# Values computed by token, modulation sums in the down-projections, operands on 2 KB lines, and the latent attention taken two heads at a time

## What is computed

```python
ckv = rms_norm(h, kv_in_norm) @ w_dkv                  # 256 latent columns and 64 rope columns
kv = rms_norm(c_kv, kv_norm) @ w_ukv                   # 8 heads of 128 key and 128 value columns
s = (q_nope @ k_nope.T + q_rope @ k_rope.T) * scale    # causal, softmax, @ v, @ w_o
```

## Time and profile before

| | |
|---|---|
| median of 3 runs | 1872.62 us (1869.66 to 1875.88) |
| the profiled execution | 1877.21 us |
| its span, first to last instruction | 1875.5 us |
| TensorE busy | 1795.5 us, 96%, 7820 matmuls |
| vector engine, ScalarE, GpSimd busy | 1142.2, 700.9, 405.1 us |
| mean granted TensorE clock | 0.979 |

### The profile page before, as it was taken

The page is one execution under the profiler, slowest core; times in us unless marked ns, Lnnn a source line. Parts: engine busy times, 40 slices in busy tenths (PEclk is TensorE's granted clock), DMA queues, the critical chain, the costliest instruction groups (busy, mean ns, idle before and its releaser), DMA issues.

```text
span 1875.5 us, 22480 instructions
## 1 busy us (share of the span) xinstructions
PE 1795.5 (96%) x7820; PEld 1422.5 (76%) x7820; DVE 1142.2 (61%) x1509; ACT 700.9 (37%) x975; POOL 405.1 (22%) x172
## 2 busy tenths in 40 slices
PE   7978999999999899999999999899999899999997
PEld 6756788888887676778888888688657688888885
DVE  6998877777224765567777522473855667777212
ACT  4112444444223335444444322332463444434221
POOL 3434300000444340120000144344201300000342
PEclk9999999999999999999999999899998899999998
DMA  7565433223333220022232233222100222232231
GB/s 266 212 212 186 172 101 100 97 93 101 101 101 98 67 93 1 32 90 94 99 100 90 97 105 101 94 89 90 56 1 13 78 90 92 98 101 89 102 101 67
DMA packets 52043, 186.32 MB, mean 99 GB/s; under 512 B 5776, under 2 KB 6032, under 8 KB 51856
## 3 DMA queue, kind: packets, MB, share of 16 engines
q1 hardware_dynamic: 50256, 180.90, 28.4%
q10 hardware_dynamic: 1728, 4.63, 0.7%
HBM read 183.41 MB, written 2.10 MB: 99 GB/s over the span
## 4 chain that ended last, share of the span: by engine, by line
PE 81%; DVE 13%; issue 2%; ACT 2%; DVEq 0%; DMA 0%; POOL 0%; ACTq 0%; SPq 0%
PE ps L1429 24%; PE ps L1431 24%; PE ps L1430 24%; DVE ada L966 4%; PE ps L1595 1%; PE ps L1592 1%; DVE TG L978 1%; PE ps L1613 1%; DVE RB L1055 1%; DVE rb L852 1%; PE ps L1649 1%; PE ps L1682 1%; PE ps L1603 1%; DVE acc L848 1%; DVE CU L990 1%
## 5 line engine op out<-in xcount | busy, mean ns | idle before, releaser
L462 POOL TENSOR_TENSOR WL<-raw,WH 128x1024 fp32r<-128x1024 f32 x159 | 394.1, 2479 | 1422.2 <-ACT WH L514 1422.2
L1429 PE MATMUL ps<-XH,WH 128*128 128x512 f32 x1560 | 616.6, 395 | 37.3 <-DVE XL L859 10.5
L1430 PE MATMUL ps<-XL,WH 128*128 128x512 f32 x1560 | 610.4, 391 | 0.0
L1431 PE MATMUL ps<-XH,WL 128*128 128x512 f32 x1560 | 610.3, 391 | 0.0
L514 ACT ACTIVATE WH<-raw 128x1024 fp32r<-128x1024 f32 x291 | 308.2, 1059 | 579.1 <-PE ps L1431 577.2
L1429 PEld LDWEIGHTS ps<-XH,WH 128*128 128x128 f32 x1560 | 294.8, 189 | 110.6 <-issue 19.5
L1431 PEld LDWEIGHTS ps<-XH,WL 128*128 128x128 f32 x1560 | 294.7, 189 | 62.2
L1430 PEld LDWEIGHTS ps<-XL,WH 128*128 128x128 f32 x1560 | 294.9, 189 | 60.9 <-issue 1.0
L1431 PE MATMUL ps<-HH,WL 128*128 128x512 f32 x528 | 208.6, 395 | 0.0
L1429 PE MATMUL ps<-HH,WH 128*128 128x512 f32 x528 | 208.6, 395 | 0.0
L1430 PE MATMUL ps<-HL,WH 128*128 128x512 f32 x528 | 208.5, 395 | 0.0
(11 more groups left out here) (257 smaller groups left out, 1877.5 us busy)
## 6 DMA issues: line engine op xcount, KB each, us to landing
raw<-w_tiles SPq DMA_DIRECT2D x291, 512.0 KB, 3.2
ada<-ada_tiles SPq DMA_DIRECT2D x48, 512.0 KB, 4.5
out_x<-X SPq DMA_DIRECT2D x8, 256.0 KB, 2.2
X<-x_in ACTq DMA_DIRECT2D x2, 512.0 KB, 8.4
X<-x_in SPq DMA_DIRECT2D x2, 512.0 KB, 8.8
MK<-mask_in ACTq DMA_DIRECT2D x1, 1024.0 KB, 4.8
crow<-c_in ACTq DMA_DIRECT2D x1, 512.0 KB, 11.5
cst<-const_in ACTq DMA_DIRECT2D x1, 384.0 KB, 13.2
```

The costliest lines, as they stand in the source:

```text
L462: nc.gpsimd.tensor_tensor(WL[k % SPL][:, :], raw[:, k, :], f32(WH[k % SPL][:, :]), ALU.subtract).then_inc(s_lo, 1)
L1429: mm(bank, h, xh, start=first, stop=False)
L1430: mm(bank, h, xl, start=False, stop=False)
L1431: return mm(bank, lo, xh, start=False, stop=last)
```

## The change

- Each value product has the activations as weights and the weight tile as the moving operand (`token_dot`, `token_group`), so that its result stands by token; `to_aux`, `turn`, `take` and `take_v` go. In UKV the first two tiles are keys, the last two values. In IN2 the first eight tiles are two groups of four banks with 512 columns, the next two (IN2R) one group of 256 columns, whose weights are read at a stride of four tokens. The four copies of a group come at its end.
- The modulation's loads and sums go to DN0 and DN1, three per chunk, in three slots; `crow` and the rope tables use other buffers and are loaded by SyncE when those are free. The operations on `mod` and `gm` follow DN1.
- The small buffers are allotted first, and the operands of the split products start on multiples of 2 KB.
- The attention takes heads 2j and 2j + 1 alternately. At an even step TensorE issues QN KN and mask of both blocks, then both rope products.

```diff
-ADA = 6
+ADA = 3
+LINE = 4 * S
-    ("IN2", 22, [1]), ("OUT2", 8, [1]), ...
+    ("IN2", 8, [0, 0, 0, 4]), ("IN2R", 2, [0, 4]), ("IN2F", 12, [1]), ("OUT2", 8, [1]), ...
-        XH = sb("XH", [P, KD, S], F32R)
+        XH = sb("XH", [P, KD, S], F32R, align=LINE)
...
-        HH = sb("HH", [P, FF, S], F32R, st)
+        HH = sb("HH", [P, FF, S], F32R, st, align=LINE)
...
+        ADA_SLOT = (ada01[:, 0, :], ada01[:, 1, :], trig[:, :, :].rearrange("p a b -> p (a b)"))
+        crow = RAB[:, :, :].rearrange("p a b -> p (a b)")
...
+        def block_a(a):
+            return a // 8 * 2 + a % 2, a % 8 // 2
...
+            def load_ada(n, m):
+                if m == 0:
+                    sp.wait_ge(s_hl, FF * (n + 1))
+                else:
+                    sp.wait_ge(s_ada, ADA * (KD * n + m))
+                for q in range(ADA):
+                    sp.dma_start(ADA_SLOT[q], ada_tiles[ADA * (KD * n + m) + q]).then_inc(s_ada_in[q], 16)
...
+                for n in range(2):
+                    down = t - T0[f"DN{n}"]
+                    if down == 5:
+                        load_ada(n, 0)
+                    elif down >= 6 and down % 3 == 0 and down <= 3 * KD:
+                        load_ada(n, down // 3 - 1)
...
             def head_hi(h):
-                act.wait_ge(s_pv, 4 * h + 4)
+                act.wait_ge(s_pv, h // 2 * 8 + 7 + h % 2)
...
-                if a % 4 == 0 and a >= 8:
-                    head_hi(a // 4 - 2)
+                if a % 8 in (3, 4) and a >= 8:
+                    head_hi(a // 8 * 2 - 2 + a % 8 - 3)
...
                     for k in range(4):
                         m, M = i * 4 + k, M0[phase] + k
+                        if modulation is not None:
+                            adaln(modulation, i, k)
                         product(M, i, per)
...
-                if a % 4 == 1 and a >= 9:
-                    head_lo(a // 4 - 2)
+                if a % 8 in (4, 5) and 8 <= a < BLOCKS_A:
+                    head_lo(a // 8 * 2 - 2 + a % 8 - 4)
+            head_lo(HEADS - 2)
             head_lo(HEADS - 1)
...
+            def token_dot(bank, t, blk, width, xh, xl, first, last):
+                h = WH[t % SPL][:, blk * width:(blk + 1) * width]
+                lo = WL[t % SPL][:, blk * width:(blk + 1) * width]
+                mm(bank, xh, h, start=first, stop=False)
+                mm(bank, xl, h, start=False, stop=False)
+                return mm(bank, xh, lo, start=False, stop=last)
...
+                if a < BLOCKS_A and a % 2 == 0:
+                    for c in (a, a + 1):
+                        h, qb = block_a(c)
+                        L, bank = (qb + 1) * P, ps[SB[c % 4]]
+                        if c >= 4:
+                            pe.wait_ge(s_p, c - 3)
+                        mm(bank[:, 0:L], QN[:, h, qb * P:L], KN[:, h, 0:L], start=True, stop=False)
+                        mm(bank[:, L - P:L], mask16[:, 0, :], mask16[:, 1, :], start=False, stop=False, ...)
+                    for c in (a, a + 1):
+                        h, qb = block_a(c)
+                        L, half, bank = (qb + 1) * P, h % 2 * HD, ps[SB[c % 4]]
+                        mm(bank[:, 0:L], QR[half:half + HD, h // 2, qb * P:L], KR[half:half + HD, 0:L],
+                           start=False, stop=True).then_inc(s_s, 1)
...
                     if qb == 0 and h >= 2:
                         pe.wait_ge(s_ol, h - 1)
...
             for k in range(n_in):
+                if k in (0, 4):
+                    token_group(T0["IN2"] + k, M0["IN2"] + k, 4, S, block_of, inputs(E_M2) if k == 0 else None)
+                elif k == 8:
+                    token_group(T0["IN2R"], M0["IN2R"], 2, 2 * P, class_of)
+                elif k >= N_TOK:
+                    wide(T0["IN2F"] + k - N_TOK, M0["IN2F"] + k - N_TOK)
```

More of the change, by code:

```diff
@@ L444, in _ @@
                 load(t)
[L445 to L448, removed]
+                if t == T0["A_OUT"]:
+                    load_crow()
+                if t == T0["UP1"] + RAW:
+                    sp.wait_ge(s_ol, HEADS)
+                    load_crow()
+                for n in range(2):
[4 more added lines that the diff above has]
+                        load_ada(n, down // 3 - 1)
+                if t == T0["DN0"] + 3 * KD + 2:
+                    sp.wait_ge(s_ada, ADA * KD)
+                    for half in range(2):
+                        sp.dma_start(trig[:, half, :], rope_in[half]).then_inc(s_in["rope"], 16)
             for m in range(KD):
@@ L599, in body @@
                         newest_tap(M + 1, i, CU, TU, jj + FF)
+                    if isinstance(i, int) and f < 2:
+                        act.wait_ge(s_in["c"], 16 * (f + 1))
+                        nc.scalar.activation(crow, crow, ACT.Silu).then_inc(s_cact, 1)
                 nc.scalar.preload_act_table(ACT.Silu)
@@ L862, in product, with adaln, residual @@
                 dve.wait_ge(s_pe, i * per + DONE_M[M])
-            def residual(phase, tiles_per_m, e, gname, n, gate=None, beside=None, second=False):
+            def adaln(n, i, k):
+                for q in range(ADA):
+                    a = i * (4 * ADA) + (ADA * (KD * n + k) + q)
+                    dve.wait_ge(s_ada_in[q], i * 64 + 16 * (KD * n + k + 1))
+                    dst = mod[:, a:a + 1] if isinstance(a, int) else mod[:, bass.ds(a, 1)]
+                    w = ADA_SLOT[q]
+                    v.scalar_tensor_tensor(w, w, 1.0, crow, ALU.mult, ALU.mult, accum_out=dst).then_inc(s_ada, 1)
+            def residual(phase, tiles_per_m, e, gname, n, gate=None, modulation=None, second=False):
                 per = 4 * tiles_per_m
@@ L1217, in in_tile @@
             def in_tile(k):
-                M, aux = M0["IN2"] + k, AUX_2 + k
-                if k < N_TOK:
-                    to_aux(aux, M)
+                M = M0["IN2F"] + k - N_TOK
+                if k in (3, 7, 9):
+                    first, dst = ((M0["IN2"], VU), (M0["IN2"] + 4, CB), (M0["IN2R"], CV12))[k // 4]
+                    for n in range(4):
+                        product(first + n)
+                        bank = ps[(first + n) % 4]
+                        v.tensor_copy(dst[:, n, :], bank[:, 0:2 * P] if k == 9 else bank[:, :]).then_inc(s_ev, 1)
+                elif k < N_TOK:
+                    pass
                 elif k < KEYS_AT:
@@ L1561, in _ @@
                         spread(1, ps[4], RA)
-                    if t > 0 and j % 2 == 0:
-                        h = 2 * (t - 1) + j // 2
-                        turn(AUX_V + h, M0["UKV"] + 2 * h + 1)
             for t in range(6):
@@ L1712, in _ @@
                 if k == KEYS_AT:
[L1713 removed]
+                    pe.wait_ge(s_ev, M0["IN2F"] + KEYS_AT - N_TOK)
                 if k >= KEYS_AT:
@@ L1717, in _ @@
             stick(BESIDE + 1)
-            pe.wait_ge(s_ev, M0["IN2"] + n_in)
+            pe.wait_ge(s_ev, M0["OUT2"])
             gated()
@@ L1847, in tiles, with rows_first @@
         return t.reshape(-1, P, TILE)
+    def rows_first(w, cols, width):
+        w = w[:, cols]
+        per = BLK * P // width
+        t = w.reshape(-1, per, P, w.shape[1] // width, width).transpose(3, 0, 2, 1, 4)
+        return t.reshape(-1, P, TILE)
     def interleave(*starts):
```

274 lines of the change are left out of this document (112 added, 162 removed).

## The result

| | before | after |
|---|---|---|
| median | 1873.84 us, 4 runs (1869.66 to 1875.88) | 1842.66 us, 4 runs (1842.36 to 1845.36) |
| the profiled execution | 1877.21 us, span 1875.5 | 1842.36 us, span 1840.6 |
| mean granted TensorE clock | 0.979 | 0.984 |

A forecast was written before the change was run, and what follows sets the result against it. TensorE, busy 96% of the span, was taken as the bound. Terms -31.8 - 10.2 - 1.3 - 3.3 - 4.8 - 3.3 + 1.3 + 6.9 = -46.5 took the profiled 1877.21 to 1830.7, the median to 1826 us; range 1813 to 1840.

The forecast's parts named there:

- Modulation: Layer A: without the vector engine's 48 multiply-accumulates, 28 tiles fall to 152.3 us, -31.8 us; DN0 and DN1 take them at 0.
- rival (d): DN0 and DN1: the moved modulation becomes a ring, at 19.4 us a chunk +93 us, kernel 1919; chance 0.02.
- Alignment: Down-projections: operands on 2 KB lines bring products from 0.233 to 0.2267 us, -10.2 us; WO -1.0, latent products -0.3.
- I take the address for the cause: Down-projections and WO: operands off 2 KB lines explain products at 0.233 us, those on XH at 0.2267.
- Rival (b): Down-projections: alignment isn't the cause of 0.233 us, but place in memory or the operands' writers; kernel 1838; chance 0.14.
- By token: UKV, UQ and IN2 lose copies and transposes: -3.3 us, ten IN2 tiles -4.8, IN2's first tile -3.3.
- The four evictions at a group's end: IN2: evictions come four at once, the next tile wants its first bank 4 us later, cost 0.
- I add 0.01 for the stride: 12.2.: IN2R: 96 half-width products with weights at stride four take 12.2 us, +1.3, bounds +0.6 and +11.7.
- rival (c): IN2R: the strided weight loads set the pace, +10.4 us, kernel 1836; chance 0.08.
- The wait for `s_ol`: Attention: TensorE waits for OL of both heads, 3.3 us at each of three changes of pair, +9.9 us.
- -3.0: Attention: back-to-back rope products each save an unhidden weight load of 0.095 us, two per pair over 16 pairs.
- rival (a): Attention: no wait for `s_ol`, 1816, or both rope products run at once, saving 4.3 us, 1812 at best; chance 0.16.

The follow-up runs named there:

- e7: Kernel before the change, with the 48 modulation products on the vector engine cut from 1024 columns to 8: 1844.03 us, two runs.
- e2: Kernel after the change, with tensors aligned to 2 KB lines moved to the next 32 bytes: 1844.44 us, ratio 0.9856.
- e5: Kernel after the change, with gaps ahead of some tensors so that some operands lie 128 bytes from the weights modulo 256: 1857.11 us.
- e1: Kernel after the change, with IN2R's stationary tile taken from 128 adjacent columns, not every fourth: 1834.94 us, ratio 0.9795.
- e11: Kernel of e4, with IN2R's stationary tile taken from every second column, not every fourth: 1817.35 us against 1828.99.
- e4: Kernel after the change, with high and low halves of a head pair's attention results made earlier: 1828.99 us, ratio 0.9766.
- e12: Kernel of e8, with the 64-row products of a head pair put apart again: 1829.82 us against 1821.23.
- e3: Kernel after the change, with attention back to one head after the other and each 64-row product in its own block: 1841.85 us.
- e6: Kernel of e4, with each block's 64-row product put back behind its own mask product: 1836.59 us against 1828.99.
- e8: Kernel of e4, with IN2R's two tiles done in two products per block instead of three: 1821.23 us, ratio 0.9732.

## Why the prediction was wrong

**Modulation, right.** -33.1 against -31.8, and e7 shows the cause: vector-engine time, not the transfers. The move into DN0 and DN1 cost nothing, as forecast; rival (d) did not come. The room there was larger than the prediction had it: a chunk is 123.1 / 8 = 15.4 us, and 15.0 after, not 14.1 and 13.6, a slip that changed no term.

**Alignment, right in size, wrong in cause.** -10.9 against -10.2. The gain came by luck: a start on a 2 KB line is not what speeds these products up, but it also puts both operands alike modulo 256. The step "I take the address for the cause" had even a wrong fact in it: by the layout given under e2 the six first buffers began 128 bytes behind a 2 KB line. e2 leaves the lines and keeps the gain, e5 takes it back with positions that differ by 128 modulo 256. Rival (b) was right to doubt the lines, and wrong to expect no gain.

**By token, nearly right.** UKV and the latent gave -3.5 against -3.6. IN2's first tile fell from 9.5 to 5.6 us (-3.9 against -3.3). The next seven gave less: TensorE waits 0.5 us in them for GpSimd's low half, and 1.2 for a bank. The four evictions at a group's end, which I had put at 0, were not free.

**The strided load: the first step that failed.** "I add 0.01 for the stride: 12.2." It is 22.5. The value stood as the upper bound, 22.6 from 0.235 each, and rival (c) is this. I took the lower one since strided passes of 64 rows had cost only 0.03 more than packed ones. I compared the passes and not the loads. The loads' own rows were in the trace of before, strided (L1691) and packed (L1595), with busy us and mean ns of one:

```profile
L1691 PEld LDWEIGHTS ps<-FT 64*128 64x128 f32 x32 | 8.6, 320 | 3.1 <-issue 1.8
L1595 PEld LDWEIGHTS ps<-KR,QR 64*128 64x128 f32 x64 | 9.4, 184 | 10.2 <-issue 10.2
```

The loads of IN2R take 330 ns, much like the strided ones here. That a load hides at a pitch of 0.11 us was true of the packed ones alone. The Trainium skill's 16-byte line (SBUF - State Buffer) spoke for the upper bound, and e1 and e11 bear it out. This step is worth 10.3 us.

**The attention: the second.** The wait for `s_ol` was there, 10.4 against 9.9, though its parts were off both ways: the first of a change of pair took 2.10 us where I had 1.5, the second 1.05 to 1.53 where I had 1.7 to 1.8. Missing was what the wait does to the clock: the earlier trace rows had 1.00 in that stretch, and I priced two idle times, of 1.5 and 1.8 us, as idle times alone. The 7.8 us are shown by e4, in which wait and fall go together. "-3.0" for the adjacent 64-row products came out at 2.9 net, by luck: they run at once, as rival (a) has it. That takes 10.2 us of work off TensorE, of which 7.4 come back as idle time. Rival (a) was also too small: it let one pass of each pair of blocks vanish, 4.3 us, and two do. I had no term for the waits for AT (4.6, before 1.2), nor for one for ScalarE (0.6). The terms add up: 10.4 + 7.8 + 3.4 + 0.6 - 10.2 = +12.0. What the pairs' order needed was another place for OH and OL: the attention 71.6 instead of 88.2 us, before 76.1.

**The sum.** By stages, -34.6 came where -46.5 was forecast. Of the 11.9 us, IN2R gives 10.3, the attention 12.0 - 6.9 = 5.1, IN2's other tiles 1.9. Against them stand layer A and the down-projections (2.0) and 3.4 in the rest of IN2, whose mean clock was 0.951 before and 0.980 after: 8.6 and 3.4 us lost at most. That the 3.4 us are the clock's doing fits e4, which has the code of after there and took 175.3 us at 0.95, nearly what before took; what moves the clock there is not shown. The medians are 3.7 us closer than the spans, since the profiled execution of before lay 3.4 above its median and that of after 0.3 below; I had taken the same 4.6 off both.

## What to carry to other kernels

Two waits on TensorE of 1 to 2 us close together can cost twice: their own length, and the products at half clock behind them. Six such waits cost 10.4 us and then 7.8; twelve of at most 1.0 us in e4 brought no fall. When an order is changed, move everything that frees a buffer with it: the same change with OH and OL one block earlier is worth 13.7 us more. Before reading fp32 weights at a stride, compare the loads' own rows, not the products': every second column cost nothing here, every fourth 10.3 us over 96 products.

## What the runs showed of the chip that I had not expected

- Products of fp32r on 512 columns come at 226.7 ns (5.44 us per 24) when both operands lie alike modulo 256 bytes, at 233 ns when they lie 128 apart (after, e2, e5, before). Leaving the 2 KB lines changed nothing (e2).
- A weight load of 128 x 128 takes 192 ns packed, 195 at every second column, 330 at every fourth, where 96 products of 256 columns came at 234 ns each (e1, e11, after).
- Two fp32 products of 64 rows and 512 columns on opposite halves of the rows take 1.06 us back to back, 2.10 with a 128-row product between them (after, e12).
- After two waits, of 2.1 and of 1.1 to 1.5 us, with a few short products between them, TensorE ran at 1.2 GHz for some 3 to 7 us (after). In e3, e6 and e12 it did for 14 us or more near the start of the stage, behind a wait of 1.3 us and some 2 us of products; after, e4 and e8 have the same wait and no fall behind it. What decides that is open.
